# Three row tiles of the modulation, moved from the norms into block two's first up projection

## The chip, the core and the metric

The kernel runs on one core of a Trainium2 chip. The metric is the device time of one execution in microseconds, taken as the median of several runs. A profiled execution gives the trace from which all rows below come.

## The reference

Two blocks of two layers each work on 256 tokens of width 1024; block two also carries 256 context tokens, which its last layer no longer updates. All arithmetic is float32. What matters here is block two:

```python
for layer in range(DEPTH):                       # DEPTH = 2
    mod = silu(c) @ w_ada[layer] + b_ada[layer]          # 1024 -> 6 * 1024
    sh1, sc1, g1, sh2, sc2, g2 = split(mod, 6)
    modc = silu(c_ctx) @ w_ada[layer] + b_ada[layer]     # the same for the context
    u  = modulate(rmsnorm(x, norm_mix_g[layer]), sh1, sc1) @ w_in[layer]
    ...
    x = x + g1 * (mixed @ w_out[layer])
    h = modulate(rmsnorm(x, norm_ffn_g[layer]), sh2, sc2)
    x = x + g2 * conv_ffn(h, w_up, conv_w, conv_b, w_down)
```

`modulate(t, shift, scale)` is `t * (1 + scale) + shift`. In `conv_ffn` the up projection gives 2 * 2816 columns, each column goes through a convolution of width three along the tokens, and `silu(a) * b` goes into the down projection. The modulation depends on `c` and `c_ctx` alone, so it may be computed at any time before it is used.

## The kernel before

**Weights as units.** All weight matrices are cut on the host into one list `ws` of units, 128 partitions by 1024 columns (768 for some), in the exact order in which the kernel uses them. `unit_widths` (L100) sets the widths and which units are plain. SyncE (L361 to 370) loads unit after unit into the ring `RAWB` with four slots (`RAW = 4`): the load of unit u waits until the unit four before it is done with. For a plain unit that is when TensorE has used it (`unit_done`), for a split unit when its lo half is written (`lo_ready`).

**Split units.** A matmul on float32 data is made of three fast ones: ScalarE copies the unit to `WHI` in the reduced format, VectorE writes the rest to `WLO` (RAWB minus WHI, L1492), and TensorE multiplies hi by hi, lo by hi and hi by lo (L509 to L511 in `fm`, L530 to L532 in `tm`). WHI and WLO have three slots each. The data side is split in the same way into NHI and NLO. ScalarE and VectorE keep a count `me.u` of the units consumed and call `split_to(me.u + 2)`: they split two units ahead (`AHEAD = 2`), counting plain units too.

**Row tiles.** The modulation's product with `w_ada` is cut into 24 tiles of 512 columns, 12 for each layer, and each tile is four plain units (`ROW_U = 4`). `rows(b)` on TensorE (L468) multiplies the 32-column operand CV2 (the two vectors c and c_ctx) with them into bank b (L480). ScalarE copies the bank to `ROWS` (`copy_rows`), `columns(b)` on TensorE turns it by 8 small matmul records into a bank (L490), and VectorE's `modulation(b)` adds `b_ada` and stores the result in MOD (L1540). The tiles are taken strictly in order, so where they stand decides only when each is computed.

**Where they stand before.** Beside block one's attention and before its output and gate projections; two tiles in the norm at the start of block one's layer 1; two in block two's mixing norm of layer 0 (one more right ahead of it) and one in that of layer 1; three and two beside the gated mixer; two in the feed-forward norm of layer 0 and one in that of layer 1.

**The norms.** TensorE sums squares into bank 4 (L552); VectorE adds the epsilon (L1527), ScalarE gives a first guess of the reciprocal root, VectorE refines it twice (L1518 to 1522). In block two VectorE then computes the factors GM (L1754), calls `ahead()`, which makes the lo halves of the two units to come, and only then runs through the eight slabs: TB (L1762), NHI on ScalarE, NLO (L1770). TensorE starts with the first slab as soon as it is split and the weights are. In block one VectorE writes Y (L1582), and NHI and NLO follow from that.

**The up projection** of block two's layer 0 is 22 pairs of units (p = 0 to 21), the two halves a and b (w = 0, 1) of the same 128 hidden columns, 24 matmuls of 512 columns each. For each unit ScalarE writes CF from the bank, VectorE adds the two outer taps of the convolution, and after a pair follow silu, the product and its split into HHI and HLO.

Of the kernel before, what the change touches and what calls it, by code (L numbers as in the profile page):

```python
# [26 lines left out]
P = 128  # L27
# [4 lines left out]
KS = D // P  # L32
DEPTH = 2
UNIT = 1024
# [61 lines left out]
GATED_ROWS = ((5, 6, 7), (5, 6))  # L96
ROW_TILES = 12


def unit_widths():  # L100
# [10 lines left out]
    for l in range(DEPTH):  # L111
        rows(2 if l > 0 else 0)
        add([UNIT] * (4 + NZ1))
        rows(4)
        add([UNIT] * (KS + 2))
        rows(1)
        add([UNIT] * KS)
    rows(1)
    for l in range(DEPTH):
        rows(2 if l == 0 else 1)  # L120
# [3 lines left out]
        rows(2 if l == 0 else 1)  # L124
        add([UNIT] * 2 * FT + [UNIT, UNIT, 6 * P] * KS)
# [24 lines left out]
def build(nc, ws, prm, cc, c1, c2, xt, ptin, mat1, bv1, wgp, nab, out):  # L150
    with ExitStack() as ctx:
# [302 lines left out]
        def _(pe):  # L454
# [157 lines left out]
            for l in range(DEPTH):  # L612
# [3 lines left out]
                else:  # L616
                    rows(5)
                    rows(6)
                    columns(5)
                tm(TT, 512, "x_split")  # L620
                if l > 0:
                    columns(6)
# [138 lines left out]
            for l in range(DEPTH):  # L761
# [3 lines left out]
                if l == 0:  # L765
                    stats(TC, SQ2)
                    columns(5)
                    rows(6)
                    rows(7)
                    columns(6)  # L770
                else:
                    rows(7)
# [275 lines left out]
        def _(act):  # L1048
# [128 lines left out]
            for l in range(DEPTH):  # L1177
# [6 lines left out]
                if l > 0:  # L1184
                    plain(2 * ROW_U)
                    first_u = me.u
                    copy_rows(5, first_u - ROW_U)
                    ahead()
                split_hi(T, Y1, 0, "t_ready")
                if l > 0:  # L1190
                    copy_rows(6, first_u)
# [94 lines left out]
            for l in range(DEPTH):  # L1286
# [8 lines left out]
                plain((2 if uc else 1) * ROW_U)  # L1295
                first_u = me.u
                if uc:
                    copy_rows(6, first_u - ROW_U)
                ahead()
                shift_hi(l, TC, SH1)  # L1300
                copy_rows(7, first_u)
# [145 lines left out]
                plain((2 if uc else 1) * ROW_U)  # L1447
                first_u = me.u
                if uc:
                    copy_rows(5, first_u - ROW_U)  # L1450
                ahead()
                shift_hi(l, n, SH2)
                copy_rows(6 if uc else 5, first_u)
                act.wait_ge(S("x_split"), me.nth("x_split", KS))

                for p in range(FT + 2):
                    if p < FT:
                        for w in range(2):
                            unit()
# [17 lines left out]
        def _(dve):  # L1477
# [99 lines left out]
            for l in range(DEPTH):  # L1577
# [6 lines left out]
                if l > 0:  # L1584
                    plain(2 * ROW_U)
# [8 lines left out]
                if l > 0:  # L1594
                    modulation(6)
# [194 lines left out]
            for l in range(DEPTH):  # L1790
# [4 lines left out]
                plain((2 if uc else 1) * ROW_U)  # L1795
# [4 lines left out]
                if uc:  # L1800
                    modulation(6)
# [531 lines left out]
```

## Time and profile before

| | us |
|---|---|
| median of 3 runs | 1683.3 |
| lowest and highest run | 1678.68, 1683.53 |
| the profiled execution's own time | 1683.68 |
| its span | 1681.6 |
| mean granted clock of TensorE in it | 0.945 of full |
| busy: PE, DVE, ACT | 1494.6, 951.1, 716.9 |

Times in rows are microseconds from the start of the span. PE is TensorE (PEld its weight loads), DVE VectorE, ACT ScalarE, SP SyncE, which issues the loads. A row of a timeline gives start and duration, engine, line and operation, output and inputs, shapes and count, and in brackets how long the engine stood idle before it and what ended that. Line 1053 is a helper through which all ScalarE operations go.

### The profile page before, as it was taken

What the parts mean: (1) busy time and instruction counts of PE and PEld (TensorE: products, weight loads), DVE (VectorE), ACT (ScalarE), POOL (GpSimd) and SP (SyncE); (2) the same over time, 40 slices, a digit from 0 to 9 for tenths busy, and PEclk for the clock granted to TensorE, in tenths of its full rate; (3) what the DMA queues carried; (4) which work ended last, traced back from release to release, by engine and by line L of the source; (5) the groups of instructions that cost most, each with busy time, mean ns of one, the idle gap of its engine ahead of it and who ended that gap; (6) DMA issues with size and microseconds to landing.
All of it is one profiled execution on the core that took longest, in us unless ns stands there. A gap on an engine that the chain in (4) does not pass through costs nothing.

```text
span 1681.6 us, 22836 instructions
## 1 busy us (share of the span) xinstructions
PE 1494.6 (89%) x9101; PEld 1249.8 (74%) x9101; DVE 951.1 (57%) x1789; ACT 716.9 (43%) x1170; POOL 71.3 (4%) x88
## 2 busy tenths in 40 slices
PE   5988887987887999978889999999979797799997
PEld 4974776973865878656568888888768774799996
DVE  4788645896545229364365655533162464488854
ACT  3435543445433255064244344322143625366642
POOL 0030000020000001200000000000000010000000
PEclk8998998998898999988989999999989898999998
DMA  5443646434535213402322233222232232455552
GB/s 208 163 138 126 224 158 229 163 127 175 189 137 180 94 63 101 173 16 70 118 101 94 95 101 100 94 94 91 72 139 85 91 111 101 152 170 181 184 185 84
DMA packets 61977, 217.52 MB, mean 129 GB/s; under 512 B 6864, under 2 KB 8912, under 8 KB 61872
## 3 DMA queue, kind: packets, MB, share of 16 engines
q1 hardware_dynamic: 59440, 206.60, 36.3%
q0 software_dynamic: 2288, 9.08, 1.7%
q8 instruction: 73, 1.20, 0.3%
q10 hardware_dynamic: 144, 0.38, 0.1%
q14 instruction: 32, 0.26, 0.0%
HBM read 214.98 MB, written 1.05 MB: 128 GB/s over the span
## 4 chain that ended last, share of the span: by engine, by line
PE 74%; DVE 13%; ACT 5%; DMA 4%; issue 4%; SPq 0%; DVEq 0%; ACTq 0%
PE bank L509 19%; PE bank L510 19%; PE bank L511 19%; DMA RAWB<-in_ws 4%; PE bank L552 2%; DVE WLO L1492 2%; PE bank L480 2%; DVE CV L1651 2%; PE bank L530 2%; PE bank L531 1%; PE bank L532 1%; DVE NLO L1770 1%; PE bank L591 1%; DVE L L1555 1%; DVE TB L1762 1%
## 5 line engine op out<-in xcount | busy, mean ns | idle before, releaser
L509 PE MATMUL bank<-NHI,WHI 128*128 128x256 f32 (+1 forms) x1808 | 597.1, 330 | 58.8 <-DVE WLO L1492 21.1
L510 PE MATMUL bank<-NLO,WHI 128*128 128x256 f32 (+1 forms) x1808 | 586.5, 324 | 0.0
L511 PE MATMUL bank<-NHI,WLO 128*128 128x256 f32 (+1 forms) x1808 | 586.1, 324 | 0.0
L1492 DVE TENSOR_TENSOR WLO<-RAWB,WHI 128x1024 fp32r<-128x1024 f32 (+1 forms) x302 | 363.0, 1206 | 331.9 <-ACT WHI L1053 329.5
L509 PEld LDWEIGHTS bank<-NHI,WHI 128*128 128x128 f32 x1808 | 351.8, 195 | 98.7 <-issue 54.5
L1053 ACT ACTIVATE WHI<-RAWB 128x1024 fp32r<-128x1024 f32 (+1 forms) x302 | 310.3, 1031 | 263.5 <-PE bank L511 175.6
L510 PEld LDWEIGHTS bank<-NLO,WHI 128*128 128x128 f32 x1808 | 352.8, 195 | 26.2 <-issue 2.2
L511 PEld LDWEIGHTS bank<-NHI,WLO 128*128 128x128 f32 x1808 | 352.4, 195 | 24.8
L1053 ACT ACTIVATE CF<-bank,PRM 128x512 f32<-128x512 f32 (+1 forms) x88 | 59.0, 671 | 185.0 <-PE bank L511 185.0
L509 PE MATMUL bank<-HHI,WHI 128*128 128x512 f32 (+1 forms) x352 | 119.6, 340 | 0.0
L510 PE MATMUL bank<-HLO,WHI 128*128 128x512 f32 (+1 forms) x352 | 118.7, 337 | 0.0
L511 PE MATMUL bank<-HHI,WLO 128*128 128x512 f32 (+1 forms) x352 | 118.6, 337 | 0.0
L2073 DVE SCALAR_TENSOR_TENSOR CF<-bank,PRM,CF 128x510 f32<-128x510 f32 (+1 forms) x88 | 54.1, 615 | 113.6 <-ACT CF L1053 112.1
L530 PE MATMUL bank<-WHI,NHI 128*128 128x384 f32 (+1 forms) x160 | 60.4, 377 | 33.5 <-issue 13.4
L480 PE MATMUL bank<-RAWB,CV 128*32 128x512 f32 x384 | 66.3, 651 | 21.9 <-DMA RAWB<-in_ws 19.9
L509 PEld LDWEIGHTS bank<-HHI,WHI 128*128 128x128 f32 x352 | 66.0, 188 | 8.5 <-DVE X L1781 0.2
L510 PEld LDWEIGHTS bank<-HLO,WHI 128*128 128x128 f32 x352 | 66.1, 188 | 8.2 <-issue 0.2
L511 PEld LDWEIGHTS bank<-HHI,WLO 128*128 128x128 f32 x352 | 66.1, 188 | 8.1
L1053 ACT ACTIVATE Z<-bank,PRM 128x256 f32<-128x256 f32 x52 | 24.6, 474 | 95.5 <-PE bank L511 95.5
L1781 DVE SCALAR_TENSOR_TENSOR X<-bank,MOD,X 128x256 f32<-128x256 f32 x48 | 21.7, 480 | 75.1 <-PE bank L511 75.1
L530 PEld LDWEIGHTS bank<-WHI,NHI 128*128 128x128 f32 x160 | 32.7, 204 | 38.1 <-issue 28.0
L1053 ACT ACTIVATE L<-L,ST 128x256 f32<-128x256 f32 (+2 forms) x68 | 37.4, 550 | 51.7 <-DVE ST L1559 51.7
(240 smaller groups left out, 1656.3 us busy)
## 6 DMA issues: line engine op xcount, KB each, us to landing
RAWB<-in_ws SPq DMA_DIRECT2D x366, 512.0 KB, 3.5
RAWB<-in_ws SPq DMA_DIRECT2D x32, 384.0 KB, 3.2
NB<-in_nab POOLq DMA_DIRECT2D x12, 256.0 KB, 3.7
K<-in_c POOLq DMA_DIRECT2D x2, 896.0 KB, 4.6
X<-in_xt SPq DMA_DIRECT2D x4, 256.0 KB, 5.0
X<-in_xt POOLq DMA_DIRECT2D x1, 1024.0 KB, 6.1
out_x<-X SPq DMA_DIRECT2D x1, 1024.0 KB, 4.8
K<-in_c POOLq DMA_DIRECT2D x1, 832.0 KB, 11.9
```

Of the source, the lines that this page charges most:

```text
L480: ins = nc.tensor.matmul(bank[b][g:g + 32, :], CV2[:, s, :], RAWB[:, u % RAW, (s % 2) * 512:(s % 2 + 1) * 512], start=(s < 4), stop=(s >= 4))
L509: nc.tensor.matmul(o, hi[:, w], xh, start=(i == 0), stop=False)
L510: nc.tensor.matmul(o, hi[:, w], xl, start=False, stop=False)
L511: ins = nc.tensor.matmul(o, lo[:, w], xh, start=False, stop=(i == slabs - 1))
L530: nc.tensor.matmul(o, xh, hi[:, c], start=(s == 0), stop=False)
L531: nc.tensor.matmul(o, xl, hi[:, c], start=False, stop=False)
L552: ins = nc.tensor.matmul(bank[4][:, 0:n], cst("ones"), sq[:, s % sq.shape[1], 0:n], start=(s == 0), stop=(s == KS - 1))
L1053: return nc.scalar.activation(out, in_, func, **kw)
L1492: V.tensor_tensor(WLO[:, k % SPL, 0:w], RAWB[:, u % RAW, 0:w], WHI[:, k % SPL, 0:w].bitcast(F32), ALU.subtract).then_inc(S("lo_ready"), 1)
L1651: ins = V.scalar_tensor_tensor(CV[:, m, :], src, w, CV[:, m, :], ALU.mult, ALU.add)
L1781: ins = V.scalar_tensor_tensor(X[:, m, w], b[:, w], MOD[:, l, gate + m, c:c + 1], X[:, m, w], ALU.mult, ALU.add)
L2073: V.scalar_tensor_tensor(y[:, :, 1:], b[:, :, :-1], prm_col(f"fw{l}", j), y[:, :, 1:], ALU.mult, ALU.add).then_inc(S("dve_chain"), 1)
```

## The change

Three row tiles change place. The norm at the start of block one's layer 1, block two's first mixing norm and block two's first feed-forward norm each have one tile instead of two (the tile right ahead of the mixing norm stays). Three tiles now stand in the up projection of block two's layer 0, at the pairs p = 4, 8 and 12, between the pair's two units: TensorE runs `rows(5)` there, and `columns(5)` behind the first unit of the next pair. The list of units follows. The order of the 24 tiles is the same, and all are still computed before they are used. Nothing else changes.

```diff
@@ unit_widths (and the same in the host's list of weights)
+UP_ROWS = (4, 8, 12)
...
-        rows(2 if l > 0 else 0)
+        rows(1 if l > 0 else 0)
...
-        rows(2 if l == 0 else 1)
+        rows(1)
         add([2 * VW] * 4 + [UNIT] * NFIRST + [2 * VW] * 4 + [UNIT] * (NZ2 - NFIRST))
...
-        rows(2 if l == 0 else 1)
-        add([UNIT] * 2 * FT + [UNIT, UNIT, 6 * P] * KS)
+        rows(1)
+        for p in range(FT):
+            add([UNIT])
+            rows(1 if l == 0 and p in UP_ROWS else 0)
+            add([UNIT])
+        add([UNIT, UNIT, 6 * P] * KS)
@@ TensorE: block one's norm, block two's mixing norm, block two's feed-forward
                     rows(5)
-                    rows(6)
                     columns(5)
                 tm(TT, 512, "x_split")
-                if l > 0:
-                    columns(6)
...
                     columns(5)
-                    rows(6)
-                    rows(7)
-                    columns(6)
-                else:
-                    rows(7)
+                rows(7)
                 tm(4, VW, "x_split")
                 columns(7)
...
                 rows(5)
-                if uc:
-                    rows(6)
-                    columns(5)
                 for m in range(2 * FT):
                     fm(KS, n, rhs, "up_freed", "x_split" if m == 0 else None)
                     if m == 1:
-                        columns(6 if uc else 5)
+                        columns(5)
+                    if uc and m % 2 == 0:
+                        if m // 2 in UP_ROWS:
+                            rows(5)
+                        if m // 2 - 1 in UP_ROWS:
+                            columns(5)
@@ ScalarE, up projection (in the norms one plain tile and one copy_rows fewer)
                         for w in range(2):
+                            if uc and w == 1 and p in UP_ROWS:
+                                plain(ROW_U)
+                                rows_u = me.u
                             unit()
...
+                        if uc and p in UP_ROWS:
+                            copy_rows(5, rows_u)
@@ VectorE, up projection (in the norms one plain tile and one modulation fewer)
                     if p == 2:
-                        modulation(6 if uc else 5)
+                        modulation(5)
+                    if uc and p - 2 in UP_ROWS:
+                        modulation(5)
                     if p < FT:
                         for w in range(2):
+                            if uc and w == 1 and p in UP_ROWS:
+                                plain(ROW_U)
                             unit()
```

TensorE at the feed-forward norm of block two's layer 0, before. L552 are the last sums of squares, L480 a row tile, L490 a column step, L509 the first matmul on the normed data:

```order
L509 MATMUL bank2<-NHI,WHI 128x512
L510 MATMUL bank2<-NLO,WHI 128x512
L511 MATMUL bank2<-NHI,WLO 128x512
L552 MATMUL bank4<-SQ2,CST 128x512 x6
L480 MATMUL bank5<-RAWB,CV2 32x512 x8
L480 MATMUL bank6<-RAWB,CV2 32x512 x8
L490 MATMUL bank5<-CST,ROWS 128x2 x4
L509 MATMUL bank3<-NHI,WHI 128x512
```

And after (the lines have moved by 5: L485 a row tile, L495 a column step, L514 the first matmul on the normed data):

```order
L516 MATMUL bank2<-NHI,WLO 128x512
L557 MATMUL bank4<-SQ2,CST 128x512 x6
L485 MATMUL bank5<-RAWB,CV2 32x512 x8
L514 MATMUL bank3<-NHI,WHI 128x512
L515 MATMUL bank3<-NLO,WHI 128x512
L516 MATMUL bank3<-NHI,WLO 128x512
```

The second row tile, into bank 6, is gone from between the sums and L509, and with it the column step that stood there.

ScalarE in the up projection at the pairs 3 and 4, before. WHI is the hi half of a weight unit, CF<-bank what it does with a finished unit, CF<-CF the silu and HHI the split of the result:

```order
L1053 ACTIVATE WHI<-RAWB 128x1024
L1053 ACTIVATE CF<-bank1,PRM 128x512
L1053 ACTIVATE WHI<-RAWB 128x1024
L1053 ACTIVATE CF<-bank2,PRM 128x512
L1053 ACTIVATE CF<-CF 128x512
L1053 ACTIVATE HHI<-CF 128x512
L1053 ACTIVATE WHI<-RAWB 128x1024
L1053 ACTIVATE CF<-bank3,PRM 128x512
L1053 ACTIVATE WHI<-RAWB 128x1024
L1053 ACTIVATE CF<-bank0,PRM 128x512
L1053 ACTIVATE CF<-CF 128x512
L1053 ACTIVATE HHI<-CF 128x512
```

And after, the same place:

```order
L1053 ACTIVATE WHI<-RAWB 128x1024
L1053 ACTIVATE CF<-bank1,PRM 128x512
L1053 ACTIVATE CF<-bank2,PRM 128x512
L1053 ACTIVATE CF<-CF 128x512
L1053 ACTIVATE HHI<-CF 128x512
L1053 ACTIVATE CF<-bank3,PRM 128x512
L1053 ACTIVATE WHI<-RAWB 128x1024 x3
L1053 ACTIVATE CF<-bank0,PRM 128x512
L1053 ACTIVATE ROWS<-bank5 128x512
L1053 ACTIVATE CF<-CF 128x512
L1053 ACTIVATE HHI<-CF 128x512
```

The WHI that stood ahead of the units in banks 2 and 3 are gone from there, and three stand in a row behind the CF of bank 3; the copy of the rows is new.

TensorE at pair 4 after the change, where before L511 of bank 3 is followed by L509 of bank 0:

```order
L515 MATMUL bank3<-NLO,WHI 128x512
L516 MATMUL bank3<-NHI,WLO 128x512
L485 MATMUL bank5<-RAWB,CV2 32x512 x8
L514 MATMUL bank0<-NHI,WHI 128x512
L515 MATMUL bank0<-NLO,WHI 128x512
L516 MATMUL bank0<-NHI,WLO 128x512
```

## Rows read from the trace of the kernel before

**Rows 1.** Chain that ended last, shares by engine and by line, from the page

```profile
PE 74%; DVE 13%; ACT 5%; DMA 4%; issue 4%; SPq 0%; DVEq 0%; ACTq 0%
```

**Rows 2.** Timeline, feed-forward norm, block two layer 0: start, us, engine, line, operation

```profile
833.13 2.23 PE L480 MATMUL bank<-RAWB,CV 128*32 128x512 f32 x8 [2.88 <-DMA RAWB<-in_ws]
...
834.25 0.18 DVE L1754 SCALAR_TENSOR_TENSOR GM<-MOD,PRM 128x16 f32<-128x16 f32 x1
...
835.60 1.05 PE L480 MATMUL bank<-RAWB,CV 128*32 128x512 f32 x4 [0.23 <-DMA RAWB<-in_ws]
...
838.48 1.06 ACT L1053 ACTIVATE WHI<-RAWB 128x1024 fp32r<-128x1024 f32 x1 [7.54 <-DMA RAWB<-in_ws]
...
840.83 1.06 ACT L1053 ACTIVATE WHI<-RAWB 128x1024 fp32r<-128x1024 f32 x1 [1.29 <-DMA RAWB<-in_ws]
...
843.06 1.67 DVE L1762 SCALAR_TENSOR_TENSOR TB<-X,GM,MS 128x256 f32<-128x256 f32 x4
...
845.94 0.76 PE L509 MATMUL bank<-NHI,WHI 128*128 128x512 f32 x1 [7.03 <-DVE NLO L1770]
```

**Rows 3.** Timeline, mixing norm, block two layer 1, with one row tile

```profile
1228.14 0.17 DVE L1754 SCALAR_TENSOR_TENSOR GM<-MOD,PRM 128x16 f32<-128x16 f32 x1
...
1230.10 1.66 DVE L1762 SCALAR_TENSOR_TENSOR TB<-X,GM,MS 128x256 f32<-128x256 f32 x4
...
1232.92 0.66 PE L530 MATMUL bank<-WHI,NHI 128*128 128x384 f32 x1 [8.78 <-issue]
```

**Rows 4.** Chain, then timeline, mixing norm, block two layer 0

```profile
508.00 3.37 DMA RAWB<-in_ws
...
512.91 0.18 DVE L1754 SCALAR_TENSOR_TENSOR GM<-MOD,PRM 128x16 f32<-128x16 f32 x1
...
520.22 1.67 DVE L1762 SCALAR_TENSOR_TENSOR TB<-X,GM,MS 128x256 f32<-128x256 f32 x4
```

**Rows 5.** Timeline, row tile ahead of the gate projection, block one, both layers

```profile
213.60 1.92 PE L480 MATMUL bank<-RAWB,CV 128*32 128x512 f32 x16
...
218.19 1.06 ACT L1053 ACTIVATE WHI<-RAWB 128x1024 fp32r<-128x1024 f32 x1 [1.97 <-DMA RAWB<-in_ws]
219.35 2.52 DVE L1492 TENSOR_TENSOR WLO<-RAWB,WHI 128x1024 fp32r<-128x1024 f32 x2 [8.19 <-ACT WHI L1053]
...
220.67 0.39 PE L509 MATMUL bank<-NHI,WHI 128*128 128x256 f32 x1 [5.14 <-issue]
...
452.28 1.92 PE L480 MATMUL bank<-RAWB,CV 128*32 128x512 f32 x16
...
459.31 0.55 PE L509 MATMUL bank<-NHI,WHI 128*128 128x256 f32 x1 [5.10 <-issue]
```

**Rows 6.** Timeline, norm of block one layer 1

```profile
254.11 3.25 DVE L1582 SCALAR_TENSOR_TENSOR Y<-X,PRM,MS 128x256 f32<-128x256 f32 x8
...
257.41 5.07 PE L480 MATMUL bank<-RAWB,CV 128*32 128x512 f32 x16 [5.16 <-DMA RAWB<-in_ws]
...
265.42 1.06 ACT L1053 ACTIVATE WHI<-RAWB 128x1024 fp32r<-128x1024 f32 x1 [1.53 <-DMA RAWB<-in_ws]
...
268.17 0.77 PE L530 MATMUL bank<-WHI,NHI 128*128 128x512 f32 x1 [4.70 <-DVE WLO L1492]
```

**Rows 7.** Stretch of the up projection: us, busy (count) by engine, PEclk, DMA, GB/s

```profile
940.00:980.00 40.00, 40.00 (x178) 33.14 (x177) 24.29 (x31) 17.92 (x24) 0.00 (x0) 1.00 0.30 99
```

**Rows 8.** Stretches behind the stalls of rows 5, and in norm of rows 3

```profile
220.67:224.20 3.53, 3.53 (x17) 3.53 (x18) 2.42 (x2) 2.34 (x2) 0.00 (x0) 0.53 0.92 308
...
456.40:463.10 6.70, 3.79 (x18) 3.82 (x19) 3.67 (x3) 4.45 (x4) 0.00 (x0) 0.50 0.89 318
...
1236.00:1238.00 2.00, 2.00 (x8) 2.00 (x7) 2.00 (x6) 1.05 (x3) 0.00 (x0) 0.50 0.00 0
```

**Rows 9.** Timeline, TensorE, column step in the up projection of block two layer 0

```profile
862.67 0.95 PE L490 MATMUL bank<-CST,ROWS 128*128 128x2 f32 x8
863.49 0.48 PE L509 MATMUL bank<-NHI,WHI 128*128 128x512 f32 x1
```

More of the change, by code:

```diff
@@ L1184, in _ @@
                 if l > 0:
-                    plain(2 * ROW_U)
-                    first_u = me.u
-                    copy_rows(5, first_u - ROW_U)
+                    plain(ROW_U)
+                    copy_rows(5, me.u)
                     ahead()
                 split_hi(T, Y1, 0, "t_ready")
-                if l > 0:
-                    copy_rows(6, first_u)
                 rest(4)
@@ L1294, in _ @@
                 guess(MS2[:, 0, :], MS2[:, 2, :], "ms_eps")
[L1295 to L1298, printed above, removed]
+                plain(ROW_U)
+                copy_rows(7, me.u)
                 ahead()
                 shift_hi(l, TC, SH1)
-                copy_rows(7, first_u)
                 act.wait_ge(S("x_split"), me.nth("x_split", KS))
@@ L1446, in _ @@
                 guess(MS2[:, 0, 0:n], MS2[:, 2, 0:n], "ms_eps")
[L1447 to L1450, printed above, removed]
+                plain(ROW_U)
+                copy_rows(5, me.u)
                 ahead()
                 shift_hi(l, n, SH2)
-                copy_rows(6 if uc else 5, first_u)
                 act.wait_ge(S("x_split"), me.nth("x_split", KS))
@@ L1458, in _ @@
                         for w in range(2):
+                            if uc and w == 1 and p in UP_ROWS:
+                                plain(ROW_U)
+                                rows_u = me.u
                             unit()
@@ L1584, in _ @@
                 if l > 0:
-                    plain(2 * ROW_U)
+                    plain(ROW_U)
                     ahead()
@@ L1593, in _ @@
                     V.tensor_tensor(V1[:, t, :], bank[t][:], BV[:], ALU.add).then_inc(S("v_freed"), 1)
-                if l > 0:
-                    modulation(6)
                 dve.wait_ge(S("ld_c1"), 16)
@@ L1794, in _ @@
                 nt = 2 * seqs
-                plain((2 if uc else 1) * ROW_U)
+                plain(ROW_U)
                 if uc:
@@ L1799, in _ @@
                 modulate(l, TC, f"nmix{l}", SH1, SC1)
-                if uc:
-                    modulation(6)
                 rest(4)
@@ L2058, in _ @@
                 stats(n, MS2)
-                plain((2 if uc else 1) * ROW_U)
+                plain(ROW_U)
                 modulate(l, n, f"nffn{l}", SH2, SC2)
-                if uc:
-                    modulation(5)
                 for p in range(FT + 2):
                     if p == 2:
-                        modulation(6 if uc else 5)
+                        modulation(5)
+                    if uc and p - 2 in UP_ROWS:
+                        modulation(5)
                     if p < FT:
                         for w in range(2):
+                            if uc and w == 1 and p in UP_ROWS:
+                                plain(ROW_U)
                             unit()
@@ L2250 @@
         w = a["w_in"][l]
-        rows(2 if l > 0 else 0)
+        rows(1 if l > 0 else 0)
         put(tm_units(w[:, v:v + 512]))
@@ L2264 @@
         w = a["w_in_2"][l]
-        rows(2 if l == 0 else 1)
+        rows(1)
         put(tm_units(w[:, v:v + VW]))
@@ L2273 @@
         tiles(a["w_out_2"][l])
-        rows(2 if l == 0 else 1)
+        rows(1)
         for m in range(FT):
@@ L2277 @@
                 put(fm_units(a["ffn_w_up_2"][l], o + m * P + np.arange(P)))
+                if l == 0 and o == 0 and m in UP_ROWS:
+                    rows(1)
         tiles(a["ffn_w_down_2"][l])
```

## The prediction

> **What bounds the kernel now.** I read the page first. In the chain that ended last TensorE holds 74%, VectorE 13% and loads 4% [rows 1]. So a change pays only where TensorE stands still, and costs wherever TensorE works without a gap. I then read the timeline at the three places that lose a row tile, and for each asked what arrives last before TensorE's first matmul on the normed data.
>
> A row tile is four plain units: the rows wait in the ring RAWB (four slots) and TensorE multiplies them with 16 matmul records in 1.9 us [rows 5], because four of them run beside each other. A column step (8 small matmuls, L490) follows somewhere behind. A weight unit needs more: its load, the hi half on ScalarE, the lo half on VectorE, and only then TensorE.
>
> In the feed-forward norm of block two's first layer the first row tile is in the ring when it is wanted. The second is not: its matmuls wait for a load until 833.13, two units' worth go from there, and the third unit follows at 835.60, so that loads land about 1.24 us apart. The two weight units behind the tile reach ScalarE at 838.48 and 840.83. VectorE has the norm's factors ready at 834.25 (GM) but begins the modulation TB only at 843.06, since it stands before the lo half of that second unit [rows 2]. The wait is on loads, not on arithmetic.
>
> **The same norm with one row tile stands in this trace**: the mixing norm of block two's second layer. There it goes from GM at 1228.14 to TB at 1230.10 with nothing but two lo halves between [rows 3].
>
> **Part 1: what the three norms give back.**
>
> Feed-forward norm, first layer: with one row tile the loads that bring row units today bring weights. They land at 833.1 and about 834.4, ScalarE needs 1.06 us for each, VectorE is free at 834.45 and needs twice 1.25 us: TB at 836.95 in place of 843.06. Gain 6.1 us. What follows is a fixed distance (843.06 to TensorE's start at 845.94) and after it the pace of VectorE's modulation, the same in both.
>
> Mixing norm, first layer: GM at 512.91, TB at 520.22 [rows 4]. The twin needs 1.96 us from GM to TB [rows 3] on units of the same 768 columns, and the first of the loads lands at 511.37, before GM. TB at 514.9, gain 5.3 us.
>
> Block one's second norm: weights now reach ScalarE in pairs ending with the unit at 265.42, and TensorE starts at 268.17, 2.75 us behind it. The first load behind the first tile lets TensorE go on at 257.41, and the next would land 1.24 us later; with one tile these two are those weight units, and 258.65 for 265.42 is 6.8 us. VectorE is done with Y at 257.36, so nothing else is later. Also the column step that now stands behind the value matmuls goes in front of them, into the idle time. A column step on the path costs 0.9 us (below). Gain 7.7 us [rows 6].
>
> What is late next is the same in all three: the lo halves of the first two weight units on VectorE, which the twin shows at its full length. Sum of the gains: 6.1 + 5.3 + 7.7 = 19.1 us.
>
> **Part 2: what a row tile costs in the up projection.** TensorE is busy for 40.00 us of every 40 there, at full clock [rows 7]; nothing covers an added step, and every microsecond goes on the end. The price has a second part that the matmul time hides. The planner splits two units ahead, and a row tile is four units, so while TensorE works on the unit before the tile there is nothing to split. The next weight unit cannot even be loaded, since all four slots hold row units and the slot it needs is freed by the tile's first two slabs. In the order after the change ScalarE has three WHI in a row behind the CF of bank 3, where now one WHI stands ahead of each unit's CF.
>
> This chain is in the trace twice, where a row tile stands ahead of block one's gate projection: the rows start at 213.60, WHI has waited for its load until 218.19, WLO starts at 219.35, and the first gate matmul at 220.67. So the tile takes 7.1 us of TensorE, of which only 1.9 are matmuls. The other layer has 452.28 to 459.31, 7.0 [rows 5]. In the up projection ScalarE and VectorE have the CF work on the unit just finished, three short steps, beside a load that lands 4.6 us behind the rows' start, so the chain is as long. The units behind it arrive about 1.2 us apart, while one takes TensorE 24 of the 178 matmuls of 40 us, 5.4 us [rows 2, 7]; there is no second stall.
>
> The half clock is the third part. In both twins TensorE resumes at the lower level of the granted clock (1.2 GHz): its mean is 0.53 over the 3.53 us behind the one stall and 0.50 over a stretch with 3.79 us of work behind the other [rows 8]. Work of 3.6 us at half the clock loses a little under half of it, 1.7 us.
>
> The column step stands on the path: 862.67 to 863.49, 0.8 us, and I take 0.9 because the first matmul behind it is drawn out (0.48 us) [rows 9]. ScalarE's copy of the rows and VectorE's MOD add lie beside matmuls, on engines with 22 and 15 of 40 us free [rows 7].
>
> Together 7.1 + 1.7 + 0.9 = 9.7 us for each tile, 29.1 us for three.
>
> **Bounds.** The stall: 7.0 to 7.2 by the twins. The clock: nothing, if the stall ends before it falls (0.53 in one twin says that it fell only as work resumed), up to 2.4 us, since in the twin norm TensorE starts at 1232.92 and the clock is still 0.50 until 1238 [rows 3, 8]; I take the gate's value, the nearest. That is 24.0 to 31.2 us for three. The norms: 16 to 20, as a lower end if loads come a little later than the row units' did.
>
> The row units' loads land 1.24 us apart, and each is 128 rows of 1024 numbers of 4 bytes, 524,288 bytes: 423 GB/s [rows 2]. The Trainium skill's page "DMA: Bandwidth & Descriptors", section "Where 436 GB/s comes from", puts the limit of a transfer from the chip's memory to SBUF at about 358 GB/s. By that rule a unit would take 1.46 us, the four units that leave each norm some 0.9 us more than I count, and the sum below would be 7.4 instead of 10.0. The trace disagrees with it at that place.
>
> **The sum.** 29.1 - 19.1 = 10.0 us more. Against the profiled execution's own 1683.68 us that is 1693.7. The median of the runs is 1683.3, 0.4 us lower, and I leave the forecast at 1693.7.
>
> **Rivals.**
>
> The clock does not fall. If the stalls of 5 us end just before it, 5.1 us fall away: 1688.6. For it: one twin kept the full clock to the end of its stall. Against it: the low level came all the same, in both. 0.10.
>
> The norms do not give back what I count. In block one's norm the loads compete with three that the GpSimd queue issues just before. If there the second weight unit lands as late as now, 6.8 us of the gain are gone: 1700.5. Against it: the first load landed by 257.41 beside the same neighbours [rows 6]. 0.10.
>
> A second stall behind each tile. VectorE must make three lo halves in a row before it may touch bank 0; if the second unit's comes late by one WLO, 1.2 us each: 1697.3. It needs VectorE to be behind, and it is busy for 24.29 of 40 us [rows 7]. 0.04.
>
> The other side: the stall is covered. If the next weight unit were split before the row tile begins, a tile would cost its 1.9 and 0.9 us alone, 8.4 us for three against 19.1 gained: 1673.0. It decides at one question, whether a slot of the ring is free for a weight unit ahead of four row units, and with exactly four slots it is not. The break-even is at 6.4 us for each tile. 0.04.
>
> **Chances.** Forecast 0.72, the rivals as given. A difference of 0.3%, 5.05 us, is about what a measurement of this kernel can tell from none. Faster: 0.04, the covered stall. Same: 0.10, the clock that does not fall. Slower: 0.86, the rest. The range goes from 1687.5 (no clock loss, and a microsecond more from the norms) to 1699.0 (clock loss of 2.4 each, and norms at 16); it leaves out the covered stall and the norm that gives nothing, 0.14 together.
>
> **What would show it.** In the profile after, VectorE should begin TB about 2 and 3 us after GM in block two's mixing and feed-forward norm, instead of 7.3 and 8.8, with no wait of TensorE for a load in either. In the up projection three gaps of about 5 us stand behind 16 row matmuls each, ended by a WLO, with a granted clock of 0.5 for some 3.6 us behind. The forecast is wrong if the gaps are absent or short, if the clock stays at 1.00 there, or if a norm still ends on a load.

## The result, and the profile after

| | before | after |
|---|---|---|
| median | 1683.2 us | 1698.1 us |
| lowest and highest of 6 runs | 1678.7, 1685.0 | 1696.3, 1701.1 |
| ratio, 95% interval | | 1.0086 [1.0074, 1.0099] |
| the profiled execution's own time, span | 1683.7, 1681.6 | 1696.3, 1694.4 |
| mean granted clock | 0.945 | 0.941 |

The changed kernel is 14.5 us slower by the ratio, 12.5 to 16.7 by its interval. The forecast was 10.0 more. I went through the three norms first, then through the three new places. All lines have moved by 5, as the section on the change says.

The page of the changed kernel, its chain that ended last by engine, and the group of row tiles (line, engine, operation, shapes, count; busy us and mean ns; idle time before, and what ended most of it):

```profile
PE 73%; DVE 14%; ACT 5%; issue 4%; DMA 4%; SPq 0%; DVEq 0%; ACTq 0%
...
L485 PE MATMUL bank<-RAWB,CV 128*32 128x512 f32 x384 | 57.4, 619 | 9.0 <-DMA RAWB<-in_ws 8.8
```

VectorE has one point more of the chain than in [rows 1], TensorE one less. Of all 384 row matmuls only 9.0 us of idle time stand before them: the rows themselves are seldom waited for. What they cost stands behind them.

The timeline of the changed kernel at the feed-forward norm of block two's layer 0, which answers to [rows 2]:

```profile
818.21 1.06 ACT L1053 ACTIVATE WHI<-RAWB 128x1024 fp32r<-128x1024 f32 x1 [1.97 <-DMA RAWB<-in_ws]
819.55 0.18 DVE L1748 SCALAR_TENSOR_TENSOR GM<-MOD,PRM 128x16 f32<-128x16 f32 x1
...
819.76 2.36 DVE L1488 TENSOR_TENSOR WLO<-RAWB,WHI 128x1024 fp32r<-128x1024 f32 x2
822.03 1.67 DVE L1756 SCALAR_TENSOR_TENSOR TB<-X,GM,MS 128x256 f32<-128x256 f32 x4
...
824.91 0.77 PE L514 MATMUL bank<-NHI,WHI 128*128 128x512 f32 x1 [9.37 <-DVE NLO L1764]
```

From GM to TB it is now 2.48 us, with two lo halves and nothing else between, where it was 8.81. The norm gives 6.3 us.

The same view at the mixing norm of block two's layer 0, which answers to [rows 4], with TensorE's next pause in the matmuls behind it:

```profile
501.61 0.17 DVE L1748 SCALAR_TENSOR_TENSOR GM<-MOD,PRM 128x16 f32<-128x16 f32 x1
...
503.56 1.67 DVE L1756 SCALAR_TENSOR_TENSOR TB<-X,GM,MS 128x256 f32<-128x256 f32 x4
...
506.39 0.66 PE L535 MATMUL bank<-WHI,NHI 128*128 128x384 f32 x1 [8.86 <-issue]
...
518.79 0.45 PE L535 MATMUL bank<-WHI,NHI 128*128 128x384 f32 x1 [2.30 <-DVE WLO L1488]
```

GM to TB takes 1.95 us, where it took 7.31: TensorE starts 5.4 us earlier in the stage. 12.40 us later it goes on behind a pause for a weight unit, as it did before the change (523.05 to 535.45); the pause is 2.30 us now and was 1.53:

```profile
535.45 0.45 PE L530 MATMUL bank<-WHI,NHI 128*128 128x384 f32 x1 [1.53 <-DVE WLO L1492]
```

And at the norm of block one's layer 1, which answers to [rows 6]:

```profile
251.98 1.05 PE L495 MATMUL bank<-CST,ROWS 128*128 128x2 f32 x8 [0.74 <-ACT ROWS L1053]
253.08 3.26 DVE L1578 SCALAR_TENSOR_TENSOR Y<-X,PRM,MS 128x256 f32<-128x256 f32 x8
...
257.56 1.06 ACT L1053 ACTIVATE WHI<-RAWB 128x1024 fp32r<-128x1024 f32 x1 [0.22 <-DMA RAWB<-in_ws]
...
260.31 0.76 PE L535 MATMUL bank<-WHI,NHI 128*128 128x512 f32 x1 [7.28 <-DVE WLO L1488]
```

From the first slab of Y to TensorE's start it is 7.23 us, where it was 14.06, so 6.8 us less. This start still hangs on a load: the second unit's WHI waited for it until 257.56, and its lo half follows at once. The column step stands at 251.98, in idle time, and its 0.9 us behind the value matmuls are gone.

At the first of the three new places, pair 4 of the up projection (the row of SPq is SyncE issuing loads):

```profile
880.73 1.92 PE L485 MATMUL bank<-RAWB,CV 128*32 128x512 f32 x16
...
881.83 6.18 SPq L375 DMA_DIRECT2D RAWB<-in_ws  x5
...
885.34 1.06 ACT L1053 ACTIVATE WHI<-RAWB 128x1024 fp32r<-128x1024 f32 x1 [3.72 <-DMA RAWB<-in_ws]
886.43 1.23 DVE L1488 TENSOR_TENSOR WLO<-RAWB,WHI 128x1024 fp32r<-128x1024 f32 x1 [3.18 <-ACT WHI L1053]
...
887.80 0.77 PE L514 MATMUL bank<-NHI,WHI 128*128 128x512 f32 x1 [5.14 <-DVE WLO L1488]
```

This is the chain of [rows 5] in a new place. The load can be issued only when the row tile has begun, and lands 4.6 us behind its start; hi and lo follow; TensorE stands for 5.14 us. The two other places have 934.40 to 941.44 and 988.49 to 995.56, so 7.0 and 7.1 us.

The granted clock around it. The windows have us, busy time of PE, PEld, DVE, ACT and POOL, then PEclk, DMA share and GB/s:

```profile
880.00:885.00 5.00, 2.66 (x20) 0.76 (x18) 1.50 (x2) 0.78 (x1) 0.00 (x0) 1.00 0.43 151
885.00:887.00 2.00, 0.00 (x0) 0.00 (x0) 0.57 (x1) 1.34 (x2) 0.00 (x0) 0.55 0.82 303
887.00:889.00 2.00, 1.20 (x3) 1.04 (x4) 1.85 (x2) 0.78 (x1) 0.00 (x0) 0.50 0.95 340
889.00:891.00 2.00, 2.00 (x6) 1.52 (x6) 0.93 (x2) 1.06 (x1) 0.00 (x0) 0.50 0.94 330
891.00:892.00 1.00, 1.00 (x4) 0.81 (x3) 0.33 (x1) 0.00 (x0) 0.00 (x0) 0.50 0.73 238
892.00:894.00 2.00, 2.00 (x10) 1.64 (x10) 0.00 (x0) 0.00 (x0) 0.00 (x0) 1.00 0.80 262
```

The clock falls to 1.2 GHz during the stall and is still there for the first 4.2 us of the work that follows. Behind the second and the third stall it is 5.2 and 5.7 us.

**The stretches of all kernels.** VectorE takes each norm's sums out of their bank with one instruction into MS (L1527 before, L1523 after; L1707 and L1701 in block one's attention). Its starts cut every kernel into the same stretches. Two rows of it in the kernel before, then in the changed one (count; shortest, median and longest duration in ns; first and last start):

```profile
L1527 DVE TENSOR_SCALAR MS<-bank x1: 691/691/691, 828.5 to 828.5; 128x512 f32<-128x512 f32 x1
L1527 DVE TENSOR_SCALAR MS<-bank x1: 691/691/691, 1222.4 to 1222.4; 128x512 f32<-128x512 f32 x1
```

```profile
L1523 DVE TENSOR_SCALAR MS<-bank x1: 691/691/691, 813.8 to 813.8; 128x512 f32<-128x512 f32 x1
L1523 DVE TENSOR_SCALAR MS<-bank x1: 693/693/693, 1233.0 to 1233.0; 128x512 f32<-128x512 f32 x1
```

So the stretch with the feed-forward norm and the three tiles takes 393.9 us before and 419.2 after. The table has these differences for all profiled executions (us; the heads give the times in the kernel before; A and D are the output and gate projections at the end of block one's layers 0 and 1, B begins with the norm that changed and has the attention of layer 1, C has block two's mixing norm and mixer of layer 0, F the feed-forward norm and the projections of layer 0, G the mixer of layer 1):

| kernel | A 166 to 250 | B to 404 | D to 489 | C 507 to 828 | F to 1222 | G to 1463 | span |
|---|---|---|---|---|---|---|---|
| before | 84.5 | 153.7 | 85.2 | 321.3 | 393.9 | 240.7 | 1681.6 |
| before, again | 84.7 | 156.1 | 83.1 | 321.4 | 393.5 | 239.0 | 1680.3 |
| after | 83.0 | 145.8 | 83.0 | 317.9 | 419.2 | 242.9 | 1694.4 |
| after, again | 82.1 | 145.6 | 85.9 | 318.3 | 419.1 | 242.9 | 1697.8 |
| norms_only | 85.2 | 145.9 | 85.0 | 315.3 | 387.6 | 237.9 | 1660.8 |
| norms_only, again | 84.5 | 146.1 | 85.1 | 315.2 | 387.6 | 240.4 | 1661.8 |
| warm | 86.0 | 146.2 | 82.9 | 319.0 | 412.0 | 242.3 | 1691.1 |
| slot5 | 84.9 | 146.1 | 83.1 | 317.8 | 405.5 | 244.1 | 1685.6 |
| slot5_early | 82.1 | 145.5 | 82.9 | 318.1 | 397.4 | 240.7 | 1669.8 |
| both_early | 77.1 | 145.4 | 79.7 | 315.3 | 396.7 | 242.4 | 1660.6 |
| gate_only | 76.9 | 153.7 | 78.7 | 321.7 | 394.3 | 241.6 | 1669.5 |
| pos_5_9_13 | 83.9 | 145.5 | 84.4 | 321.2 | 418.8 | 240.1 | 1697.3 |
| one_tile | 83.6 | 154.1 | 86.0 | 321.6 | 398.1 | 243.6 | 1690.7 |

### The profile page after: what moved, and what is told of

Its sections match the earlier page's. It is cut to its first block, busy times and chain, and to the rows that moved or that the text cites. A ratio compares the mean times of both kernels' runs of the same rounds, so it can differ in the third digit from the quotient of the medians.

```text
span 1694.4 us, 22836 instructions
## 1 busy us (share of the span) xinstructions
PE 1493.4 (88%) x9101; PEld 1254.5 (74%) x9101; DVE 949.8 (56%) x1789; ACT 718.8 (42%) x1170; POOL 71.3 (4%) x88
## 4 chain that ended last, share of the span: by engine, by line
PE 73%; DVE 14%; ACT 5%; issue 4%; DMA 4%; SPq 0%; DVEq 0%; ACTq 0%
PE bank L514 19%; PE bank L516 18%; PE bank L515 18%; DMA RAWB<-in_ws 4%; DVE WLO L1488 2%; PE bank L557 2%; DVE CV L1645 2%; PE bank L535 2%; PE bank L536 2%; PE bank L537 2%; PE bank L485 1%; DVE NLO L1764 1%; DVE L L1551 1%; PE bank L596 1%; DVE TB L1756 1%
## 5 line engine op out<-in xcount | busy, mean ns | idle before, releaser
L514 PE MATMUL bank<-NHI,WHI 128*128 128x256 f32 (+1 forms) x1808 | 599.2, 331 | 74.9 <-DVE WLO L1488 34.3
L514 PEld LDWEIGHTS bank<-NHI,WHI 128*128 128x128 f32 x1808 | 352.5, 195 | 118.5 <-issue 75.7
L514 PE MATMUL bank<-HHI,WHI 128*128 128x512 f32 (+1 forms) x352 | 119.6, 340 | 0.0
L514 PEld LDWEIGHTS bank<-HHI,WHI 128*128 128x128 f32 x352 | 66.0, 188 | 8.4 <-DVE X L1775 0.2
L485 PE MATMUL bank<-RAWB,CV 128*32 128x512 f32 x384 | 57.4, 619 | 9.0 <-DMA RAWB<-in_ws 8.8
L536 PE MATMUL bank<-WHI,NLO 128*128 128x384 f32 (+1 forms) x160 | 59.2, 370 | 0.0
```

What stands on the lines that cost most here:

```text
L485: ins = nc.tensor.matmul(bank[b][g:g + 32, :], CV2[:, s, :], RAWB[:, u % RAW, (s % 2) * 512:(s % 2 + 1) * 512], start=(s < 4), stop=(s >= 4))
L514: nc.tensor.matmul(o, hi[:, w], xh, start=(i == 0), stop=False)
L536: nc.tensor.matmul(o, xl, hi[:, c], start=False, stop=False)
```

## The experiments

**The theory** is the prediction's own: a row tile takes all four slots of the ring, so the next weight unit is loaded, split and only then used, 5.1 us of stall; the clock falls in the stall; a norm with one tile less gives back what its loads took. The rivals were another mechanism behind the stall (the place, or what ScalarE and VectorE have to do there), a clock that costs nothing, and norms that give less than counted.

**norms_only.** The norms as after the change, without the three tiles: 3 of the 24 row tiles are not computed, and their part of the modulation is set to zero.

```diff
-UP_ROWS = (4, 8, 12)
+UP_ROWS = ()
```

> The changed kernel without its three row tiles in the up projection: the norms have one tile each, and three of the 24 row tiles are not computed at all (their part of the modulation is set to zero). Theory 1, the loads of the second tile were what each norm waited for: 19.1 us below the kernel before by the prediction's sum, 17 to 19 if the value matmuls of the mixing norm again lose some 1.6 us to the clock as in the profile after; 1664 to 1666. The tiles in the up projection then cost the rest, about 33 us. Theory 2, the norms give back much less and the up projection costs the predicted 29.1: the difference to the changed kernel is 29, so about 1669, 14 below the kernel before.

Measured 1662.4 us, ratio 0.9874 [0.9859, 0.9889] to the kernel before, 21.2 us less (18.7 to 23.8). Stretch F is 387.6 us, 6.3 below the kernel before and 31.6 below the changed one: 10.5 us for each tile. That two profiles of it have 387.6 twice, and two of the changed kernel 419.2 and 419.1, makes this the firmest number of the study. Stretch B is 8.6 us shorter in the nine profiles with the new norm (mean 145.8) than in the four with the old one (154.4), stretch C with the some 18 us ahead of it 3.8 us (335.5 against 339.3). One of the four old B is 156.1 us, the others 153.6 to 154.0; without it the difference in B is 8.0.

By the medians the three tiles cost more than stretch F shows: 21.2 and 14.5 us are 35.7, 11.9 for each tile, against 31.6. The changed kernel is also longer than this one in stretches without a tile, C (317.9 and 318.3 for 315.3 and 315.2) and G (242.9 twice for 237.9 and 240.4).

**warm.** The changed kernel with 18 matmuls behind each row tile, whose result nobody reads, so that TensorE has work until the next unit is split. Left out here is one wait ahead of the projection, until their bank is free.

```diff
...
+                            for d in range(18):
+                                nc.tensor.matmul(bank[6][:, :], NHI[:, d % KS, 0:P], NHI[:, d % KS, :], start=True, stop=True)
```

> The changed kernel with 18 idle matmuls of 512 columns (4.1 us at full clock) behind each row tile of the up projection, into a bank that nobody reads; the weights' way is untouched, so the gap to the next weight matmul stays 7.1 us. If the clock's fall in the gap costs 2.0 to 2.5 us for each tile (granted clock 0.50 for 4.2 to 5.4 us in the profile after), the time goes down by 6 to 7.5 us, to about 1691, and the granted clock behind the tiles is 1.00. If the clock costs only the predicted 1.7 each, 1693. If it costs nothing, 1698.

Measured 1689.3 us, ratio 1.0038 [1.0025, 1.0050]: 8.8 us less than the changed kernel by the medians, 8.1 by the ratios. Its timeline on TensorE at pair 4, and the windows there:

```profile
885.26 1.92 PE L485 MATMUL bank<-RAWB,CV 128*32 128x512 f32 x16
887.11 4.42 PE L1043 MATMUL bank<-NHI 128*128 128x512 f32 x18
892.28 0.47 PE L514 MATMUL bank<-NHI,WHI 128*128 128x512 f32 x1 [0.75 <-DVE WLO L1492]
```

```profile
887.00:892.00 5.00, 4.53 (x22) 3.30 (x18) 1.84 (x2) 1.95 (x2) 0.00 (x0) 1.00 0.91 323
892.00:894.00 2.00, 1.72 (x8) 1.45 (x9) 1.36 (x2) 1.14 (x2) 0.00 (x0) 1.00 0.88 322
```

The chain behind the row tile has its full length, 885.26 to 892.28, 7.0 us. Only the clock has changed: 1.00 throughout. Stretch F loses 7.2 us, 2.4 for each tile, and that is the price of the clock, with useless work in its place.

**slot5.** The first unit of each row tile in the up projection goes to a buffer of its own (4 KB more for each partition), so that the ring has a slot for the weight unit behind the tile. What the engines do, and in which order, is as in the changed kernel.

```diff
+            if l == 0 and p in UP_ROWS:
+                SPECIAL.append(len(w))
...
+RING_UNITS = [u for u in range(NU) if u not in SPECIAL]
+RING_NO = {u: i for i, u in enumerate(RING_UNITS)}
...
-                sp.dma_start(RAWB[:, u % RAW, 0:w], ws[u, :, 0:w]).then_inc(S(f"raw{u % RAW}"), 16)
+                sp.dma_start(raw(u, 0, w), ws[u, :, 0:w]).then_inc(S(raw_sem(u)[0]), 16)
```

> The changed kernel with one more buffer of 4 KB for the first plain unit of each up projection row tile, so that the ring also holds the next weight unit before the tile begins; the planner is unchanged and still splits that unit only behind the last CF. The load is out of the chain, ScalarE's and VectorE's work is left: WHI to about 2.0 us, WLO behind VectorE's two steps to about 3.7 us from the rows' start. The gap goes from 5.1 us to about 1.9, the clock should stay: 3 x (3.3 + 2.3) = 17 us less than the changed kernel, about 1681. Rival, the stall is the planner's and not the ring's: no change, 1698.

Measured 1683.4 us, ratio 1.0002 [0.9989, 1.0016], the same as the kernel before. Its timeline at pair 12:

```profile
982.53 0.62 PE L514 MATMUL bank<-RX,CV 128*32 128x512 f32 x2
...
983.32 1.04 ACT L1082 ACTIVATE WHI<-RAWB 128x1024 fp32r<-128x1024 f32 x1
...
984.97 1.22 DVE L1517 TENSOR_TENSOR WLO<-RAWB,WHI 128x1024 fp32r<-128x1024 f32 x1
986.33 0.47 PE L543 MATMUL bank<-NHI,WHI 128*128 128x512 f32 x1 [1.88 <-DVE WLO L1517]
```

WHI no longer waits for a load. What stands between the rows and TensorE is now ScalarE's CF, WHI, and VectorE's taps ahead of WLO: 1.88 us of stall in place of 5.1. In stretch F a tile costs (405.5 - 387.6) / 3 = 6.0 us.

The expectation had the clock stay, and the time near 1681. It did not stay everywhere: behind two of the three stalls of 1.88 us it is at 0.50 for 3.4 us, at pair 4 (the first row) and at pair 12 (the two others), and behind the one at pair 8 it is at 1.00:

```profile
888.66:892.07 3.41, 3.41 (x10) 2.65 (x9) 1.83 (x2) 2.12 (x2) 0.00 (x0) 0.50 0.94 356
...
986.00:990.00 4.00, 3.67 (x12) 2.95 (x12) 1.41 (x2) 1.28 (x2) 0.00 (x0) 0.71 0.78 268
990.00:994.00 4.00, 4.00 (x17) 3.31 (x16) 1.23 (x1) 1.18 (x2) 0.00 (x0) 0.87 0.91 330
```

Twice 1.7 us lost is 1.1 for each tile; with 3.8 us from the rows to TensorE's start and 0.9 for the column step that makes 5.8 of the 6.0.

**slot5_early.** The same, and ScalarE and VectorE split the weight unit behind the tile one unit earlier, before the row tile begins.

```diff
                         for w in range(2):
+                            if uc and w == 0 and p in UP_ROWS:
+                                split_to(me.u + ROW_U + 2)
```

> As slot5, and ScalarE and VectorE split that weight unit one unit earlier, before the row tile begins. Then a tile costs its matmuls and its column step alone, 1.9 + 0.9 us, 8.4 us for three: by the prediction's rival of the covered stall 1673, 10 us below the kernel before. If the early split only moves the wait to another place (ScalarE late for a CF, VectorE late for a bank), 1675 to 1681.

Measured 1675.8 us, ratio 0.9957 [0.9936, 0.9977]. In stretch F a tile costs (397.4 - 387.6) / 3 = 3.3 us. The rows and the windows behind them at pair 8:

```profile
926.84 0.62 PE L514 MATMUL bank<-RX,CV 128*32 128x512 f32 x2
...
928.69 0.50 PE L543 MATMUL bank<-NHI,WHI 128*128 128x512 f32 x1
```

```profile
926.00:930.00 4.00, 4.00 (x26) 1.89 (x26) 1.75 (x3) 0.78 (x1) 0.00 (x0) 1.00 0.27 65
930.00:934.00 4.00, 4.00 (x19) 3.31 (x18) 0.58 (x1) 1.06 (x1) 0.00 (x0) 1.00 0.83 301
```

There is no gap, and the clock stays at 1.00. This is the covered stall, the rival of the other side, made by hand: the same move of three tiles, and the kernel is faster than before. In the change as it stands the slot is missing.

**gate_only and both_early.** The prediction took its price from the two row tiles ahead of block one's gate projection. gate_only is the kernel before with those two tiles treated as in slot5_early; both_early is slot5_early with them.

```diff
+        SPECIAL.append(len(w))
...
                         for u in range(2):
+                            if u == 1:
+                                split_to(me.u + ROW_U + 2)
```

> The kernel before with nothing changed but the two row tiles ahead of the gate projection, treated as in both_early. Theory 1: 1684.6 - 13.6 = 1671.0 us, and no stall behind either tile. Theory 2: 1678 us or more. If the two effects are independent, the difference to the kernel before is that between both_early and slot5_early.

> slot5_early, and the same treatment (first unit of the row tile in a buffer of its own, 4 KB more, and the weight unit behind the tile split before it) for the row tile ahead of block one's gate projection in both layers. Theory 1 (every row tile ahead of a weight unit costs 5.1 us of stall and some 1.7 us of half clock because the ring holds no weight unit): the two twins that the prediction rested on lose 6.8 us each, 1675.8 - 13.6 = 1662.2 us. Theory 2 (in the gate stage something else is late as soon as the stall is gone, for example the normed slabs on VectorE): less than half of that, 1669 us or more.

gate_only: 1672.2 us, ratio 0.9930 [0.9915, 0.9945], 12.1 us less. both_early: 1665.7 us, ratio 0.9895 [0.9877, 0.9913], the fastest kernel here that computes everything, 18.6 us below the kernel before. It is 10.1 below slot5_early by the medians; the theory said 13.6. TensorE in gate_only behind the tile of layer 0, and the windows of both layers:

```profile
210.97 0.62 PE L508 MATMUL bank<-RAWB,CV 128*32 128x512 f32 x2
...
213.05 0.36 PE L537 MATMUL bank<-NHI,WHI 128*128 128x256 f32 x1 [0.17 <-issue]
```

```profile
211.00:216.00 5.00, 4.83 (x42) 3.36 (x42) 1.23 (x1) 1.88 (x4) 0.00 (x0) 1.00 0.54 188
...
443.00:448.00 5.00, 4.84 (x42) 3.23 (x41) 1.23 (x1) 1.92 (x4) 0.00 (x0) 1.00 0.50 170
```

The stalls of 5.1 us are gone in both layers and the clock does not fall behind the tiles. Stretch A is 7.7 us below the mean of the kernel before, stretch D 5.4. Theory 2's figure, less than half of 13.6, is excluded, but theory 1's 13.6 was too much by 1.5 us in gate_only and by 3.5 in both_early. A wait that the old kernel does not have stands in both layers, some 5.2 us behind the first gate matmul:

```profile
218.21 0.35 PE L537 MATMUL bank<-NHI,WHI 128*128 128x256 f32 x1 [1.27 <-DVE WLO L1522]
...
450.54 0.36 PE L537 MATMUL bank<-NHI,WHI 128*128 128x256 f32 x1 [1.24 <-DVE WLO L1522]
```

A later unit's lo half is late there: 2.5 us for the two layers, and 1.19 and 1.26 us at the same places in both_early. Something else is late once the stall is gone, as theory 2 had it, but only for a quarter of the stall. The two kernels should have gained the same if the repairs were independent; they gained 12.1 and 10.1, and why they differ is not shown.

**pos_5_9_13.** The three tiles one pair later.

```diff
-UP_ROWS = (4, 8, 12)
+UP_ROWS = (5, 9, 13)
```

> The changed kernel with its three tiles one pair later (p = 5, 9, 13). Theory 1 (the price is that of the chain rows, free slot, load, hi, lo, and the same at any place in the projection): within 2 us of the changed kernel, 1696 to 1700 us, three gaps of 5.1 us. Theory 2 (the places 4, 8 and 12 are unlucky, by what ScalarE and VectorE have to do there): another time by more than 3 us.

Measured 1698.3 us, ratio 1.0074 [1.0051, 1.0098]; stretch F 418.8 us; stalls of 5.15, 4.98 and 5.08 us. The place does not matter, at least not between these two sets of pairs.

**one_tile.** The kernel before with one tile moved, from the feed-forward norm to pair 8.

```diff
-UP_ROWS = (4, 8, 12)
+UP_ROWS = (8,)
```

> The kernel before with one tile alone moved: the second of block two's feed-forward norm goes to the up projection at p = 8, all else as before. Theory 1 by the rows of both profiles (gain of the norm 6.3, tile 10.5): 4.2 us more, 1688.8 us. By the medians of the first runs (35.7 us for three tiles, 11.9 each): 5.6 us more, 1690.2. By the prediction's own terms (6.1 and 9.7): 3.6 us more, 1688.2. Theory 2 (the tiles are dear only together, through the clock or the order of the units): no more than 2 us above the kernel before.

Measured 1688.8 us (12 runs), ratio 1.0028 [1.0017, 1.0040], 4.6 us more than before. Stretch F has 398.1 us, 4.2 to 4.6 more than the two profiles of before. A single move loses already, by 10.5 - 6.3 = 4.2; the tiles are not dear only together.

**before_again, after_again, norms_only_again.** Three kernels profiled a second time, nothing edited. Stretches of unchanged code had differed by up to 6.2 us between kernels (column G), and I wanted to know whether the kernel or the execution does that.

> The kernel before, profiled a second time. The stretch from the sums of the last mixing norm to those of block two's last feed-forward norm (1222.4 to 1463.1 us, the same code in every kernel so far) took 240.7 us here, and from 237.9 to 244.1 us in the other kernels. Theory 1 (where the granted clock falls in a stretch varies from one execution to the next): this stretch and the one from 165.9 to 250.4 (84.5 us) come out different by 1 to 3 us from the first profile. Theory 2 (it is fixed by what each kernel did before): both within 0.5 us of the first profile.

> The changed kernel, profiled a second time. Its first profile has 242.9 us for the stretch behind the sums of the last mixing norm and 83.0 us for block one's gate stage. Theory 1 (varies by execution): different by 1 to 3 us. Theory 2 (fixed by the kernel): within 0.5 us. The stretch with the three tiles, 419.2 us in the first profile, should stay within 1 us under both.

> The changed kernel without the three tiles of the up projection (3 of 24 row tiles not computed), profiled a second time. It had the shortest such stretch, 237.9 us, and 85.2 us for block one's gate stage. Theory 1 (varies by execution): nearer to the 240 to 244 us of the others. Theory 2 (fixed by the kernel): 237.4 to 238.4 us again.

Stretch G: 239.0 for 240.7, 242.9 for 242.9, 240.4 for 237.9. Stretch D: 83.1 for 85.2, 85.9 for 83.0, 85.1 for 85.0. Stretch A moved by 0.2, 0.9 and 0.7, and B by 2.4 in the kernel before. So it varies by execution, as theory 1 said, though not in every stretch: by nothing to 2.9 us. Stretch F moved by 0.4, 0.1 and 0.0. No run was made to set what makes A, B, D and G vary, but in A and D it goes with the granted clock. Stretch D in the kernel before, and in its second profile:

```profile
404.06:489.31 85.25, 73.46 (x544) 64.34 (x546) 44.79 (x78) 42.40 (x70) 0.00 (x0) 0.94 0.54 185
406.91:490.00 83.09, 71.61 (x544) 62.48 (x546) 44.70 (x79) 42.40 (x70) 0.00 (x0) 0.98 0.56 190
```

Over the eleven profiles with the old row tile there, a mean clock of 0.98 has 82.1 to 83.1 us in either stretch, 0.96 has 83.7 to 84.7, 0.94 has 84.9 to 85.3 and 0.92 has 85.8 to 86.0. A, B, D and G are stretches in which TensorE often stands still (204 us of PE in 240.7 of G, at a mean clock of 0.92), while in F it hardly does.

## Why the prediction was right, and where a size was off

The forecast was 1693.7 us in a range of 1687.5 to 1699.0; the median was 1698.1. Side and mechanism were right, the size was 10.0 for 14.5, and the median lies 0.9 us inside the upper end of the range.

**What bounds the kernel, and the waits.** Right. All three norms ended on loads, and with one tile less the lo halves of the first two units are what is late in block two's norms, as the twin of [rows 3] has it. In block one's norm that sentence of the prediction does not hold to the letter: its start still hangs on the second weight unit's load, only 6.8 us sooner, which is how its gain was counted. In the up projection the three gaps are there, each ended by a WLO, with rows before and the lower clock behind.

**The feed-forward norm.** 6.1 predicted, 6.3 measured (393.9 to 387.6).

**Block one's norm.** 7.7 predicted; 6.8 and the column step by the timeline, 8.6 by the mean of stretch B (8.0 without the one long B). The rival that GpSimd's loads delay the second weight unit fell: the two WHI stand 1.28 us apart.

**The mixing norm.** 5.3 predicted, 5.4 at TensorE's start, but over the stretch the changed kernel keeps only some 3.2 (335.6 and 336.2 in its two profiles, 339.2 and 339.0 before). The step that failed is that what follows TensorE's start is the same in both kernels; the prediction says it of the feed-forward norm and uses it here. The pause 12.40 us behind the start is not the same: it was 1.27 to 1.87 us in the four profiles with the old norm, and with the new norm it is 1.93 to 1.96 in three and 2.15 to 2.37 in six. In the three, stretch C is 315.2 to 315.4 and the whole gain is there (5.6 us, 333.7 against 339.3); in the six it is 317.7 to 321.2. The windows of the changed kernel show what the longer pause brings, a clock that falls behind it; in norms_only (the third row, pause of 1.95 us) it does not:

```profile
515.00:520.00 5.00, 2.70 (x16) 2.38 (x15) 3.90 (x8) 3.44 (x5) 2.54 (x4) 1.00 0.21 56
520.00:525.00 5.00, 5.00 (x22) 5.00 (x21) 0.74 (x1) 0.12 (x1) 1.00 (x2) 0.66 0.95 347
...
524.00:529.00 5.00, 5.00 (x29) 5.00 (x30) 1.95 (x2) 1.08 (x2) 2.22 (x3) 1.00 0.91 309
```

In the kernel before the clock is 1.00 from 530 to 540, around its pause. The other traces agree without exception: the clock falls behind the pause in those six and in none of the seven others, and 30 matmuls behind the pause TensorE is 19.3 us from its start in the six and 17.7 in the seven, 1.6 us lost. The pause always ends at the same distance, so its length says how early TensorE reaches it: the granted clock is back at 1.00 some 3.3 us behind TensorE's start in the changed kernel (pause 2.30 us), 4.0 in norms_only (1.95) and 5.0 in the kernel before (1.53). In six of the nine profiles with the faster norm part of its gain is thus lost again. No edit was made that sets the pause or the clock alone, and the three profiles differ from the six already ahead of the norm (17.7 to 17.9 us between the sums of D's end and those of C, and 18.4 to 18.5 in the three). So where the time goes is shown, and what puts an execution into one group or the other is open.

**The tile: 9.7 predicted, 10.5 measured.** The stall and the rows were 7.1 and measured 7.0 to 7.1; one_tile and pos_5_9_13 have 6.9 to 7.1. The column step of 0.9 stands. The term that was too small is the clock: 1.7 predicted, 2.4 measured by warm. The prediction counted 3.6 us of work at the lower level from the gate's stretches, and it was 4.2, 5.2 and 5.7; half of that is 2.5 on average, and 7.1 + 2.5 + 0.9 is the 10.5 of stretch F. It had the right value as a bound, 2.4, from the norm of [rows 3 and 8], and took the other because its stall was of the same kind. With 2.4 the sum would have been 12.1.

**The sum.** 31.6 for the tiles less 6.3, 8.6 and 3.8 gives 12.9 us more by stretches, inside the interval of 12.5 to 16.7 that the runs give. From 10.0 to 12.9 the tiles add 2.5 and the mixing norm 1.5, and the two other norms, which gave more than counted, take 1.1. Of the 1.6 us that remain to 14.5, stretch G shows a candidate. It begins with a mixing norm too, and both profiles of the changed kernel fall into the group with the longer pause there, neither of the kernel before. The next pause that all kernels share stands 22.73 us behind TensorE's start in the kernel before (start at 1232.92) and 24.32 in the changed one (start at 1243.50):

```profile
1255.65 0.50 PE L509 MATMUL bank<-NHI,WHI 128*128 128x512 f32 x1 [0.94 <-ACT V L1053]
...
1267.82 0.50 PE L514 MATMUL bank<-NHI,WHI 128*128 128x512 f32 x1 [0.94 <-ACT V L1053]
```

That is 1.6 us in code that nobody changed; slot5 has it as well, the ten other profiles do not. Stretch G is 242.4 us on average in the eight profiles with tiles in the up projection and 239.9 in the five without, but the two ranges overlap (240.1 to 244.1, 237.9 to 241.6). Whether the moved tiles bring it about or the execution does is not shown.

**The rivals.** The clock that does not fall: no, and warm shows its price, 1689.3 against the 1688.6 that the prediction gave for that case, though by other sizes. The second stall: no, the second WHI at 886.72 and its WLO at 887.81 are in time for a unit that TensorE wants 7 us later. The covered stall: not in this change, but slot5_early made it, at 1675.8 for 1673.0. Its break-even of 6.4 us for each tile agrees with slot5, where a tile costs 6.0 and the kernel is as fast as before.

**The loads.** The limit in the Trainium skill (page "DMA: Bandwidth & Descriptors", section "Where 436 GB/s comes from") does not show after the change either: the two WHI of block one's norm stand 1.28 us apart on units of 524,288 bytes, 410 GB/s, where that page's some 358 GB/s would give 1.46 us.

## What to carry to other kernels

Filler work in an idle gap is priced by what it pushes out of the buffers, not by its own matmuls: here 1.9 us of rows cost 10.5, since they took every slot of the ring and the next weight unit could be neither loaded nor split. Before moving such work into a busy loop, ask whether the next unit's load and its split can run ahead of it; one spare buffer and one earlier split brought a tile from 10.5 to 3.3 us, and the same repair at two old places was worth 10 to 12 us. And a stall on TensorE costs more than its length, since the work behind it runs for some microseconds at half clock; take that price from the row with continuous work behind the stall.

## What the runs showed of the hardware

The clock did not fall at once in a stall: of the 5.1 us without work from 882.7 to 887.8, the stretch to 885 is at 1.00 and only 885 to 887 has 0.55. What costs is the lower level behind it, 4.2 to 5.7 us of full work, in which a matmul of 512 columns follows the other every 0.43 us instead of every 0.23. Eighteen matmuls with no use in each of three gaps, 4.42 us of work, kept the clock up and made the kernel 8.1 us faster by the ratios (7.2 in stretch F). Short stalls can bring the lower level too: 3.4 us of it stood behind two of slot5's three stalls of 1.88 us, and behind nine of the 26 pauses of 0.98 to 2.37 us in block two's mixing norms, the longer ones, where it cost 1.6 us each.

Stretches of identical code differ by up to 2.9 us between two executions of one kernel where TensorE often pauses, and by no more than 0.4 us where it works through. In block one's gate stretches the difference goes with the granted clock (85.25 us at 0.94, 83.09 at 0.98). A comparison of two profiles says little below 3 us for the first kind, and tenths of a microsecond for the second.
